# Layer 0 and 1 projections of the first block in rounded parts, w_ada chunks loaded ahead of x, 16 row blocks moved among the gates

## The reference

```python
for l in range(2):
    mod_lat = (silu(c) @ w_ada[l] + b_ada[l])              # 6 x 1024: sh1 sc1 gt1 sh2 sc2 gt2
    mod_ctx = silu(c_ctx) @ w_ada[l] + b_ada[l]
    h   = rms_norm(x, g_attn[l]) * (1 + sc1) + sh1         # the same for ctx with its own mod
    p   = h @ w_in[l]                                      # gates 2048, c_q 768, c_kv 256, k_r 32, na 3 x 512
    mq  = rms_norm(rms_norm(c_q) @ w_uq)                   # 8 heads of 96
    k_nope, mv = split(rms_norm(c_kv) @ w_ukv)             # 8 heads of 64 + 64
    mk  = rms_norm(concat(k_nope, k_r)); nq, nk = rms_norm(na[0]), rms_norm(na[1]); nv = na[2]
    y_mla = attention(rope(mq), [mk_ctx, rope(mk)], [mv_ctx, mv])
    y_na  = neighbourhood_attention(nq, nk, nv, nk_ctx, nv_ctx, rpb)
    x  += gt1 * ((sigmoid(g1) * (y_mla @ w_mla_o) + sigmoid(g2) * (y_na @ w_na_o)) @ w_out)
    x  += gt2 * (square(relu(h2 @ w_ff1)) @ w_ff2)         # h2: norm and modulation again
```

## Time and profile before

| | us |
|---|---|
| median of 3 runs (2174.6 to 2181.35) | 2174.66 |
| profiled execution | 2173.98 |
| its span, first to last instruction | 2172.2 |
| PE busy, 94% of the span | 2045.1 |
| DVE busy, 60% | 1298.3 |
| ACT busy, 40% | 873.3 |
| POOL busy, 1% | 15.2 |

### The profile page before, as it was taken

The page is one execution under the profiler, slowest core; times in us unless marked ns, Lnnn a source line. Parts: engine busy times, 40 slices in busy tenths (PEclk is TensorE's granted clock), DMA queues, the critical chain, the costliest instruction groups (busy, mean ns, idle before and its releaser), DMA issues.

```text
span 2172.2 us, 28152 instructions
## 1 busy us (share of the span) xinstructions
PE 2045.1 (94%) x10952; PEld 1595.4 (73%) x10952; DVE 1298.3 (60%) x2333; ACT 873.3 (40%) x1541; POOL 15.2 (1%) x32
## 2 busy tenths in 40 slices
PE   6999998999989999999999999999999999999987
PEld 2445434478868888885575488999999888999877
DVE  2555666654467767773235656666676575676674
ACT  2223344544333323222244455544443454443552
POOL 0000000000000000000000000000000000000000
PEclk9999999999999999999999999999999999999999
DMA  8332320022235454433212045444444223444323
GB/s 321 109 148 84 131 97 1 1 97 85 97 110 177 172 179 151 174 136 129 71 41 97 1 156 186 179 174 174 150 172 146 99 98 136 162 159 136 107 68 107
DMA packets 49554, 272.61 MB, mean 126 GB/s; under 512 B 5648, under 2 KB 6800, under 8 KB 27664
## 3 DMA queue, kind: packets, MB, share of 16 engines
q1 hardware_dynamic: 45392, 238.50, 31.0%
q0 software_dynamic: 4032, 32.31, 4.0%
HBM read 269.74 MB, written 1.05 MB: 125 GB/s over the span
## 4 chain that ended last, share of the span: by engine, by line
PE 75%; DVE 11%; ACT 8%; issue 5%; DMA 1%; ACTq 0%; SPq 0%; DVEq 0%
PE bank L480 14%; PE bank L516 13%; PE bank L482 13%; PE bank L481 13%; PE bank L689 4%; PE bank L682 3%; ACT w_parts L1078 2%; DVE small_lo L1475 2%; PE bank L527 1%; PE bank L552 1%; PE bank L605 1%; PE bank L931 1%; PE bank L933 1%; PE bank L932 1%; DVE stat L1449 1%
## 5 line engine op out<-in xcount | busy, mean ns | idle before, releaser
L1478 DVE TENSOR_TENSOR w_parts<-ring,w_parts 128x2048 fp32r<-128x2048 f32 x96 | 219.8, 2291 | 103.9 <-ACT w_parts L1078 103.9
L480 PE MATMUL bank<-h_parts,w_parts 128*128 128x512 f32 (+1 forms) x768 | 263.3, 343 | 14.4 <-DVE h_parts L1734 7.1
L481 PE MATMUL bank<-h_parts,w_parts 128*128 128x512 f32 (+1 forms) x768 | 261.4, 340 | 0.0
L482 PE MATMUL bank<-h_parts,w_parts 128*128 128x512 f32 (+1 forms) x768 | 261.3, 340 | 0.0
L1078 ACT ACTIVATE w_parts<-ring 128x2048 fp32r<-128x2048 f32 x96 | 182.8, 1907 | 175.4 <-PE bank L482 175.4
L516 PE MATMUL bank<-h,ring 128*128 128x512 f32 (+2 forms) x624 | 224.6, 519 | 7.0 <-ACT h L1115 7.0
L480 PE MATMUL bank<-b_parts,w_parts 128*128 128x512 f32 (+1 forms) x640 | 215.7, 337 | 1.5 <-DVE w_parts L1478 1.1
L481 PE MATMUL bank<-b_parts,w_parts 128*128 128x512 f32 (+1 forms) x640 | 215.0, 336 | 0.0
L482 PE MATMUL bank<-b_parts,w_parts 128*128 128x512 f32 (+1 forms) x640 | 215.0, 336 | 0.0
L480 PE MATMUL bank<-h_hi,small_hi 128*128 128x256 f32 x704 | 205.8, 292 | 6.4 <-DVE small_lo L1475 5.3
L1475 DVE TENSOR_TENSOR small_lo<-ring,small_hi 128x1024 fp32r<-128x1024 f32 x138 | 163.7, 1207 | 70.4 <-ACT small_hi L1067 69.8
(11 more groups left out here) (236 smaller groups left out, 3689.2 us busy)
## 6 DMA issues: line engine op xcount, KB each, us to landing
ring<-in_w SPq DMA_DIRECT2D x140, 1024.0 KB, 4.8
ring<-in_w SPq DMA_DIRECT2D x152, 512.0 KB, 3.5
lowrank<-in_rows POOLq DMA_DIRECT2D x24, 1024.0 KB, 5.1
lowrank<-in_bias POOLq DMA_DIRECT2D x2, 2048.0 KB, 9.6
ring<-in_w SPq DMA_DIRECT2D x4, 864.0 KB, 4.4
x<-in_x SPq DMA_DIRECT2D x1, 2048.0 KB, 8.9
lowrank<-in_con POOLq DMA_DIRECT2D x1, 1856.0 KB, 9.8
ring<-in_w SPq DMA_DIRECT2D x2, 800.0 KB, 4.3
```

Source lines behind the costliest of these rows:

```text
L480: pe.matmul(ps, w[0][:, k, :], hi, start=k == 0, stop=False)
L481: pe.matmul(ps, w[0][:, k, :], lo, start=False, stop=False)
L482: return pe.matmul(ps, w[1][:, k, :], hi, start=False, stop=k == nk - 1)
L1478: dve.tensor_tensor(w_parts[pair][:, 1, 0:size], ring[:, slot, 0:size], w_parts[pair][:, 0, 0:size].bitcast(F32), ALU.subtract).then_inc(* ...
```

## The change

- Kinds: cq, ckv, kr, nq, nk, nv become rounded small chunks (kind 3), row, uk, uv, uq plain small chunks (kind 2). There is no kind 0 any more, and the slots change between small and big at each change of stage. kr is loaded with the 64 columns ahead of it.
- h is kept in parts: ACT writes `h_hi1` (where yT was), DVE `h_lo1` (in h's place). The gates read h_hi1; in the na tiles DVE only copies h_lo1 to h_parts. The y heads go to tmp and sq, yg_hi to h_parts' place.
- The first three cq tiles are computed together, k by k. Layer 1 makes the parts of x's columns first, then those of ctx, with the rounding of cq 4 and 5 between.
- The 8 w_ada chunks of the start have their own tensor `ada` in wide, three loaded ahead of x, five behind it. c_rows comes from PE: ones times 16 diagonal matrices made by DVE.
- 16 row blocks stay in the projections (8 up to nk, 8 in mq), 16 go to the gates, two behind each n, with loads of 512 KB on POOL's queue into prob's two halves. late_modulation(0) goes behind the gates.
- At the end of layer 0's MLP ACT and DVE round the first four cq chunks of layer 1.

```diff
-AFTER = {("cq", 1): 1, ("cq", 3): 1, ("cq", 5): 1, ("ckv", 1): 1, ("nq", 0): 1, ("nq", 2): 2, ("nk", 0): 1,
-         ("nk", 2): 2, ("uk", 3): 1, ("nv", 0): 1, ("uq", 0): 1, ("uq", 3): 2, ("uq", 6): 1}
+AFTER = {("cq", 4): 1, ("ckv", 0): 1, ("kr",): 1, ("nq", 1): 1, ("nq", 3): 1, ("nk", 1): 1, ("nk", 3): 1, ("uk", 3): 1,
+         ("uq", 0): 1, ("uq", 1): 1, ("uq", 2): 1, ("uq", 3): 1, ("uq", 4): 1, ("uq", 5): 1, ("uq", 6): 1, ("uq", 7): 1}
+ROWS = 2 * FIRST + 16
+GROUP = 3
-PLAIN2 = ("memk", "memv")
-SPLIT2 = ("dt", "xbc", "rq", "rk", "sq", "sk", "mq", "rv", "sv", "gate", "out2")
+PLAIN2 = ("memk", "memv", "row", "uk", "uv", "uq")
+SPLIT2 = ("cq", "ckv", "kr", "nq", "nk", "nv", "dt", "xbc", "rq", "rk", "sq", "sk", "mq", "rv", "sv", "gate", "out2")
...
+            def nv_tile(l, i, t):
+
+                ps = next_bank("nv", l, i, t, until=("v_copied", "nv", l, i, t))
+                for a in range(2):
+                    w = split_weights(("nv", l, i, a))
+                    for k in range(4):
+                        hi, lo = (v[:, 4 * a + k, P * t:P * t + P] for v in (h_hi1, h_lo1))
+                        pe.matmul(ps[:, 0:256], hi, w[0][:, k, :], start=4 * a + k == 0, stop=False)
+                        pe.matmul(ps[:, 0:256], hi, w[1][:, k, :], start=False, stop=False)
+                        mm = pe.matmul(ps[:, 0:256], lo, w[0][:, k, :], start=False, stop=4 * a + k == KT - 1)
+                full(mm, "nv", l, i, t)
...
+                banks = [next_bank("cq", l, i, until=("copied", "cq", l, i)) for i in range(GROUP)]
+                group_w = [split_weights(("cq", l, i)) for i in range(GROUP)]
+                for k in range(KT):
+                    pe.wait_ge(*event("h_lo", "n1", l, k))
+                    last = [split_product(banks[i][:, 0:cw], group_w[i], k, h_hi1[:, k, t0:TT], h_lo1[:, k, t0:TT], KT)
+                            for i in range(GROUP)]
+                for i in range(GROUP):
+                    full(last[i], "cq", l, i, more=i < GROUP - 1)
...
-            sp.dma_start(x[:, :, :], dram["x"]).then_inc(*signal("x_in", by=16))
+            for j in range(FIRST):
+                if j == 3:
+                    sp.dma_start(x[:, :, :], dram["x"]).then_inc(*signal("x_in", by=16))
+                if j > 3:
+                    sp.wait_ge(*event(f"ada_in{j % 4}", j - 4))
+                sp.dma_start(ada[:, j, :, :], dram["ada"][j]).then_inc(*signal(f"ada_in{j % 4}", j, by=16))
...
+                def norm1():
+                    dve.wait_ge(*event("rs", "n1", l))
+                    r = given("rs", ("n1", l))
+                    todo = streams(l)
+                    for j in range(len(todo) + 1):
+                        if j in (KT + 1, KT + 4):
+                            split_weights(("cq", l, 4 + j // (KT + 4)), 1)
+                        if j < len(todo):
+                            k, _, both = todo[j]
+                            for s in both:
+                                cols = slice((1 - s) * TC, (1 - s) * TC + TC)
+                                ins = dve.scalar_tensor_tensor(h[:, k, cols], x[:, k, cols], amp[:, 0, k, s:s + 1],
+                                                               r[:, cols], ALU.mult, ALU.mult)
+                            ins.then_inc(*signal("scaled", "n1", l, j))
+                        if j:
+                            k, _, both = todo[j - 1]
+                            dve.wait_ge(*event("h_hi", "n1", l, j - 1))
+                            for s in both:
+                                cols = slice((1 - s) * TC, (1 - s) * TC + TC)
+                                ins = dve.scalar_tensor_tensor(h_lo1[:, k, cols], h[:, k, cols], mod(l, s)[:, k:k + 1],
+                                                               h_hi1[:, k, cols].bitcast(F32), ALU.add, ALU.subtract)
+                            ins.then_inc(*signal("h_lo", "n1", l, j - 1))
...
                 for name, n, c0 in (("cq", 6, t0), ("ckv", 2, 0)):
                     for i in range(n):
+                        split_weights((name, l, i), 3)
                         copy(name, l, i, heads1[name][:, i, c0:TT])
                         if name == "cq" and i > 1:
                             add_square("cq", l, i - 1, cw)
-                        row_blocks(1)
+                        if (name, i) in (("cq", 3), ("cq", 5), ("ckv", 1)):
+                            row_blocks(1)
...
                     if g[0] == "na" and 4 <= u < 4 + KT:
-                        low_part(h_parts, u - 4, h[:, u - 4, t0:TT], slice(t0, TT), "h", "h", l)
+                        dve.tensor_copy(h_parts[:, 1, u - 4, t0:TT], h_lo1[:, u - 4, t0:TT]).then_inc(*signal("h_lo", "h", l, u - 4))
...
                     merge("g1", "mo", n)
                     if n:
                         low_yg(n - 1)
+                    row_blocks(2)
                 merge("g2", "no", KT - 1)
                 low_yg(KT - 1)
+                if l == 0:
+
+                    late_modulation(0)
+                    gains(1, "g_mlp")
...
                         split_weights(("ff2", l, g, n))
-                        if (l, g, n) == (L - 1, NG - 1, KT - 1):
-                            split_weights(("sq", 0, 0), 1)
+                        if (g, n) == (NG - 1, KT - 1):
+                            split_weights(("sq", 0, 0) if l else ("cq", 1, GROUP), 1)
                         residual(n, 40, "x_mlp", "ff2", l, g, n)
```

More of the change, by code:

```diff
@@ L81, in weight_entries @@
     out = []
-    late = [FIRST]
+    late = [2 * FIRST]
     def add(key, src, l, k0, nk, cols):
@@ L342, in program, with split_end @@
         slots = ring_slots(chunks)
+        def split_end(key, ahead):
+            i = place[key][0]
+            if slots[i][0] == 1:
+                return min(i + ahead, next(j for j in range(i, len(slots)) if slots[j][0] != 1))
+            end = next((j for j in range(i, len(slots)) if slots[j][0] == 1), len(slots))
+            return ([j for j in range(i, end) if slots[j][0] == 3][0:ahead] or [i])[-1] + 1
         def loaded(i):
@@ L1054, in _ @@
             split_next = {"at": 0}
+            l_now = [0]
             def split_weights(key, ahead=2):
-                for i in range(split_next["at"], min(place[key][0] + ahead, len(slots))):
+                for i in range(split_next["at"], split_end(key, ahead)):
                     kd, slot, _, pair, before = slots[i]
@@ L2092, in lay_out @@
         block(("row",), "w_ada", 1, 0, KT, range(256 * j, 256 * j + 256)) for j in range(ADA)]))
[L2093 removed]
+    ada = np.ascontiguousarray(np.stack([
+        a["w_ada"][0][:, 256 * j:256 * j + 256].reshape(KT, P, 256).transpose(1, 0, 2) for j in range(FIRST)]))
+    rows0 = np.ascontiguousarray(np.stack([
+        block(("row",), "w_ada", 0, 0, KT, range(P * b, P * b + P)) for b in range(ROWS, 48)]))
+    return {"w": w, "par": par, "rows": rows, "rows0": rows0, "ada": ada, "bias": bias, "mem": feature_major(a["mem_2"][0]),
             "x": feature_major(np.concatenate([a["ctx"][0], a["x"][0]])), **constants()}
```

282 lines of the change are left out of this document (148 added, 134 removed).

## The result

The changed kernel takes 2141.45 us (median of 4 runs, 2139.49 to 2143.95) against 2175.75 of the kernel before beside it: ratio 0.984, 95% interval 0.982 to 0.986, some 34 us less. The forecast was 2136, the range 2119 to 2157. The profiled execution of after is its slowest, 2143.95 (span 2142.2); of before it was the fastest, 2173.98.

What follows compares the result with a forecast made beforehand. PE was taken to bound the projections and gates, a DVE/ACT loop layer 0's mq; the stage terms summed to -38.8 us from 2173.98, giving 2135.2, forecast as 2136 us with the median's 0.7, range 2119 to 2157.

Steps and rivals of the forecast that it cites:

- (b): Hand-over paces more stages, narrow tiles in layer 1 and every second tile in layer 0; 2156 us, chance 14%.
- (c): Slower: rounding of 42 chunks lies open before each tile, 94 us against 56.5 of gain; 2212 us, chance 4%.
- (a): All of PE's saving arrives, 56.5 us with the casts; 2118 us, chance 12%.
- cq to kr of layer 0: Layer 0's first projections: PE paces, nine wide tiles save 1.43 us each, -12.9 us.
- the second block: Code behind the first block keeps its instructions, so no change: 0 us.
- Spacing: Rounded matmuls follow each other at 0.226 us for 512 columns and 0.12 for 256, read from the kernel's own rows.
- the gates: Layer 0's gates: 16 added row blocks make low parts late, 0.4 us four times and 1.3 at the end; +3 us.
- into layer 1: End of layer 0's MLP: four low parts ahead of residual 7 delay layer 1's first matmul, +3.4 us.
- layer 1's cq to kr: ckv 0 rounded last in line, PE waits 5.6 us, then runs slow; -1.2 us where PE's arithmetic promises 7.7.
- mq's loop: Layer 0's mq: a DVE/ACT loop of 7.05 us per head sets the pace and stays, 0 us.
- Start: Up to the first projection matmul: loads pace, PE's eighth product ends at 41.5, earlier gain is spent again; +0.7 us.
- Softmax: ACT's casts of h go, DVE's become copies of 0.43 to 0.69 us; -4 us in layer 0, -1 in layer 1.

Runs made afterwards that it cites:

- gates_end: Changed kernel with the last two of the gates' 16 row blocks moved behind low_yg(7); ratio to the kernel before 0.9833.
- trans: Changed kernel with low parts of layer 1's first four cq chunks split two and two ahead of residuals 6 and 7, two row blocks moved earlier; ratio to before 0.9794.
- late_first: Changed kernel with layer 1's eight late halves of h made before cq 4, cq 5 and ckv 0 are rounded; ratio to the kernel before 0.9804.
- rows_out: Changed kernel with mq's eight row blocks moved to layer 0's out, one per n, late_modulation's last columns behind out; ratio to the kernel before 0.9867.

## Why the prediction was right, and where its terms were off

- **What bounds.** Right: in layer 0's projections PE paced and got faster by the matmuls' arithmetic, -13.2 and -10.5 for -12.9 and -11.4. The lookahead of two or three chunks covered the 2.25 us of rounding. Rivals (b) and (c) fall there: PE is busy 53.5 of 54.2 us in layer 0's nq and nk. Rival (a) falls in layer 1, where cq to kr saved nothing.
- **Right by luck: cq to kr of layer 0.** Nine tiles at the measured spacing save 9 x (6.87 - 5.60) = 11.4, not 12.9. The other 1.8 is the first tile: in before it took 8.64 us at a clock of 0.80, behind 3.47 us of idling; in after PE idles only 0.65, behind the c_row products, and the clock is full. The prediction had left out what this wait cost before. Before, then after:

```profile
51.69:60.33 8.64, 8.64 (x17) 3.71 (x18) 5.68 (x13) 7.35 (x16) 0.00 (x0) 0.80 0.00 2
```

```profile
50.67:55.00 4.33, 4.33 (x19) 3.51 (x20) 4.33 (x12) 2.31 (x6) 0.00 (x0) 1.00 0.00 0
```

- **Left out: the second block**, 0 for +6.7, the largest miss. The prediction followed the new lookahead through layer 1 and took what comes behind for unchanged. The order of roundings there changed, and one place costs 4 to 6 us; the rest, some 2, is no more than executions differ by themselves.
- **Spacing.** 0.226 was read from a stretch whose operands stand right to each other; the projections ran at 0.2333. Over 408 matmuls of layer 0 that is 2.7 us. The rule weighed beside it (the Trainium skill, "TensorE: Matmul & The Clock Gate", Back-to-back issue gap: N/2.4 + 2.5 ns between warm matmuls taken singly, 216 at 512 columns) has no place for either: rounded passes take 0.2267 at best.
- **Mis-sized: the gates**, +3 for +5.1. The waits were near what was worked out (three of 0.37 in the middle for four of 0.4, and the 1.30 at the end, which gates_end takes away). The other 2.7 is again spacing: 552 matmuls x 0.0049 on average, because g1 and g2 now read h_hi1 from yT.
- **Mis-sized: into layer 1**, +3.4 for +5.2. The low parts cost their 3 us (trans); the slow sum of squares, 3.75 for 1.96 us, was left out, though the earlier trace rows had shown what such a wait does.
- **Mis-sized: layer 1's cq to kr**, -1.2 for +2.4. The order of events was right, the wait ahead of ckv 0 was 5.3 for 5.6, but the cq tiles took 2.3 longer, the slow stretch lasted 1 us longer, spacing took 0.5. late_first shows that nearly all of it, and some 7 us more, hung on the order of roundings and halves in the queues.
- **Wrong step: mq's loop.** The rows gave 7.05 us per head and a chain of DVE and ACT of the same sum; I took it for the pace of the stage. The sign came true and still misled: in after DVE's last copies are 7.04 apart (243.20, 250.24, 257.28), but PE's heads 6.73. Only DVE's end is later by it, 1 us in all (rows_out). The -2.9 measured is something else: in before PE waited 3.04 us at 266.16, and after has no such wait. The row names no releaser; loads run from 262 to 268, so it was most likely for a weight chunk, gone with the new loads. This row, of the kernel before, I had not read:

```profile
266.16 4.07 PE L516 MATMUL bank<-lowrank,ring 128*96 128x512 f32 x9 [3.04 <-issue]
```

- **Start.** +0.7 for -1.0: the loads did not pace (PE's eighth product ended at 40.1, not 41.5), and the c_row products kept PE at work ahead of the first tile.
- **Softmax.** -4 for -5.0. The cast became 0.42 us, as the row within SBUF had it; the upper end 0.69 falls:

```profile
L1735 DVE CAST h_parts<-h_lo 128x512 fp32r<-128x512 f32 x8 | 3.4, 419 | 0.1
```

Between the two profiled executions the sum is -30.0 for -38.8. The misses do not all point one way: the second block, the way into layer 1, its cq to kr and the gates took some 14 us more than forecast, and mq, the start, mk and nv (1.2, not traced) and the softmax gave nearly 7 back. That the median lies only 5 us from the forecast owes something to this. What decides in which execution the clock falls behind the same wait stays open.

## What to carry to other kernels

In a queue worked off in order, ask of each instruction that waits for a buffer what could run in that wait: the same work in another order gave some 10 us, its amount did not matter. When the meaning of a helper's argument changes, compare the queues at every place that calls it, also where nothing else changed. Price a wait of PE with what comes behind it: two waits of 5.3 us cost 1.8 and 2.9 us more at the lower clock. When an operand moves to another tensor, compare the spacing of the matmuls that read it, not only who waits.
